# Scan of a state-space mixer: z projection between the heads, decays from running sums, norms per group

## The reference, cut to what matters

```
proj = u @ w_in                    # 256 x 5152: z 2048, xbc 3072, dt 32
xbc = silu(causal_dwconv(xbc, conv_w, conv_b))
xs, bm, cm = 32 heads x 64, 4 groups x 128, 4 groups x 128
dt = softplus(dt_raw + dt_bias);  a = -exp(a_log)
cs = cumsum(dt * a)                # per head, over time
y[l] = sum over s <= l of (cm[l] . bm[s]) * exp(cs[l] - cs[s]) * dt[s] * xs[s]
y = y + d_skip * xs
g = y * silu(z), normed by its mean square in each of 4 groups of 512
return (g * norm_w) @ w_out        # 2048 -> 1024
```

## Time and profile before

| what | value |
|---|---|
| median of 3 runs | 2651.09 us (2650.17 to 2657.0) |
| profiled execution | 2655.34 us, span 2653.6 us |
| PE busy | 2250.7 us, 85% of the span |
| DVE busy | 885.7 us, 33% |
| ACT busy | 364.8 us, 14% |
| DMA | 638 MB, 240 GB/s over the span |
| mixer, first z matmul to the last of the output product | 1501.32 to 1784.97 us |

### The profile page before, as it was taken

One profiled execution on the slowest core, in us unless ns is written; L12 is line 12 of the kernel. 1 busy time (PEld: TensorE's weight loads), 2 busy tenths in 40 slices (PEclk: granted clock), 3 DMA queues, 4 the chain that ended last, 5 costly groups with the idle time before them and its releaser, 6 DMA issues.

```text
span 2653.6 us, 28827 instructions
## 1 busy us (share of the span) xinstructions
PE 2250.7 (85%) x11598; PEld 1591.9 (60%) x11598; DVE 885.7 (33%) x1985; ACT 364.8 (14%) x740; POOL 1.2 (0%) x16
## 2 busy tenths in 40 slices
PE   6999999976666666667666799999999988899998
PEld 4877888832222222222222588687888877788886
DVE  6895994131000000100000226715231325333223
ACT  2231111120000000000000111302110114111111
POOL 0000000000000000000000000000000000000000
PEclk9999999988887788888878899999999989999999
DMA  7526563549999999999999742044444421454420
GB/s 267 178 96 213 200 223 126 236 195 429 427 428 429 429 428 430 428 429 429 429 429 428 266 159 96 1 142 143 159 158 146 142 98 62 155 175 147 157 95 16
DMA packets 147181, 638.03 MB, mean 240 GB/s; under 512 B 10245, under 2 KB 52750, under 8 KB 119198
## 3 DMA queue, kind: packets, MB, share of 16 engines
q1 hardware_dynamic: 146158, 634.79, 61.1%
q10 hardware_dynamic: 944, 2.13, 0.2%
HBM read 635.86 MB, written 1.05 MB: 240 GB/s over the span
## 4 chain that ended last, share of the span: by engine, by line
PE 69%; DMA 23%; DVE 5%; ACT 1%; issue 1%; SPq 0%; ACTq 0%; DVEq 0%
DMA arena<-in_w_down_dram 23%; PE PS L1520 17%; PE PS L1034 12%; PE PS L1533 8%; PE PS L947 8%; PE PS L1372 4%; PE PS L1274 3%; PE PS L1363 2%; PE PS L1399 2%; PE PS L958 2%; PE PS L1386 2%; DVE arena L1609 2%; PE PS L1282 1%; DVE rstd L1618 1%; PE PS L1466 1%
## 5 line engine op out<-in xcount | busy, mean ns | idle before, releaser
L1372 PE MATMUL PS<-arena,hT 128*32 128x512 f32 x2048 | 310.0, 749 | 163.7 <-DMA arena<-in_w_up_dram 137.9
L1520 PE MATMUL PS<-hT,arena 128*128 128x256 f32 x2048 | 444.5, 379 | 2.9 <-DVE hT L1609 2.9
L1520 PEld LDWEIGHTS PS<-hT,arena 128*128 128x128 f32 x2048 | 388.9, 190 | 56.6 <-issue 3.8
L1372 PEld LDWEIGHTS PS<-arena,hT 128*32 128x32 f32 x2048 | 66.8, 126 | 386.4 <-DMA arena<-in_w_up_dram 211.7
L1034 PE MATMUL PS<-hT,arena 128*128 128x256 f32 (+1 forms) x1136 | 253.7, 383 | 1.5 <-ACT hT L682 1.5
L1386 PE MATMUL PS<-arena,hT 128*32 128x512 f32 x1024 | 170.7, 804 | 98.2 <-DMA arena<-in_w_down_dram 90.3
L1609 DVE SCALAR_TENSOR_TENSOR arena<-arena 128x512 f32<-128x512 f32 (+2 forms) x514 | 246.5, 548 | 0.9
L1034 PEld LDWEIGHTS PS<-hT,arena 128*128 128x128 f32 (+1 forms) x1136 | 213.4, 190 | 39.4 <-issue 9.7
L1533 PE MATMUL PS<-arena 128*128 128x256 f32 x1024 | 223.3, 379 | 0.0
L1606 DVE TENSOR_SCALAR arena<-arena,cols 128x256 f32<-128x256 f32 x162 | 66.4, 410 | 465.0 <-ACT arena L879 380.4
L947 PE MATMUL PS<-hT,arena 128*128 128x256 f32 x960 | 214.0, 387 | 6.1 <-DVE hT L1609 6.1
(11 more groups left out here) (242 smaller groups left out, 1627.6 us busy)
## 6 DMA issues: line engine op xcount, KB each, us to landing
arena<-in_w_gate_dram SPq DMA_DIRECT2D x64, 2048.0 KB, 40.8
arena<-in_w_up_dram SPq DMA_DIRECT2D x64, 2048.0 KB, 40.7
arena<-in_w_down_dram SPq DMA_DIRECT2D x64, 2048.0 KB, 37.5
arena<-in_ffn_w_up_dram SPq DMA_DIRECT2D x32, 2048.0 KB, 8.7
arena<-in_w_in_dram SPq DMA_DIRECT2D x36, 1024.0 KB, 8.0
arena<-in_ffn_w_down_dram SPq DMA_DIRECT2D x16, 2048.0 KB, 8.0
arena<-in_w_ada_dram SPq DMA_DIRECT2D x12, 2048.0 KB, 11.6
arena<-in_ssd_w_in_dram SPq DMA_DIRECT2D x10, 2048.0 KB, 12.8
```

The source lines that it names most:

```text
L1372: mm = pe.matmul(PS[32 * f:32 * f + 32, 1 + half, :], xe[:, 32 * (2 * pi + k):32 * (2 * pi + k) + 32], w[:, k, 512 * f:512 * f + 512], sta ...
L1520: mm = pe.matmul(PS[:, n, T * half:T * half + T], slot(TAIL_SLOT[j], 8, 512)[:, k, P * n:P * n + P], hT[:, k, :], start=(k == 0), stop=(k ...
```

## The change

The order of the weights is dt, x, z, and so is PE's. dt comes first; dt, da and their running sums are made beside the x tiles. The tiles of x and z go through three PSUM banks instead of four (`ssd_tile`); the transposes of xs follow four by four behind the panels (`x_turn`), and so do their products with dt (`x_dt`). Running sums of da over time are made once, by five products with the triangular constant: `cs` with tokens on partitions, `csT` with the 32 heads twice on 64 partitions.

The heads run in 16 pairs. `decay` broadcasts the row of `csT` of each of the two heads over 128 partitions, by one product on 32 rows with a column of the identity as stationary operand, the two heads on different rows. `span` on DVE subtracts the other running sum and takes the minimum with zero, from PSUM into `em`; ACT takes exp of a pair at once, `weigh` on DVE multiplies a pair with `cb`; the masks are in `cb`. `head_out` does the two heads of a pair in turn, first both products of 256 columns and then both of 128. Between the decays of a pair and the output of the pair two before, PE has one z tile; ACT copies it out and takes silu of four together. Norm and squares of a group follow within the loop or, for group 3, within the output product, which now uses banks 0 to 3 and starts before the last two outputs of pairs. The norm behind the mixer changes its banks accordingly.

```diff
@@ -96,7 +96,7 @@
...
-TAIL = [("ssd_z", 4), ("ssd_dt", 1), ("ssd_x", 6), ("ssd_out", 4), ("ffn0", 25), ("lru_in", 5),
+TAIL = [("ssd_dt", 1), ("ssd_x", 6), ("ssd_z", 4), ("ssd_out", 4), ("ffn0", 25), ("lru_in", 5),
...
 def norm_bank(name):

-    return 3 if "post" in name or name in ("lat_q", "ffn1") else 7
+    if name == "ssd3":
+        return 4
+    return 3 if "post" in name and name != "mix_post0" or name in ("lat_q", "ffn1", "ssd0", "ssd1", "ssd2") else 7
...
-        td = [sq_[:, 384 * i:384 * i + 384] for i in range(4)]
-        em = [oa_[:, 384 * i:384 * i + 384] for i in range(3)]
+        em = [view(so_, 1024 + 768 * i, 2, 384) for i in range(3)]
+        csT, da2 = so_[0:64, 3328:3584], view(so_, 3584, 2, 64)
+        cs = view(so_, 3712, 2, SSD_H)
...
+            def z_copy(t):
+                act.wait_ge(*tile_done(s, used, "z_ps", ["ssd_x", "ssd_z"], NX + t))
+                act.activation(zs[:, t, :], PS[:, t % 3, 0:T], ACT.Copy).then_inc(s["z_ready"], 1)
+            def group_squares(g):
+                act.wait_ge(s["ss_ps"], NORM[f"ssd{g}"][0])
+                squares(f"ssd{g}", lambda p, n: zs[:, 4 * g + 2 * p:4 * g + 2 * p + 2, :],
+                        lambda p: ("yg_ready", 4 * g + 2 * p + 2))
+            z_copy(0)
+            for i in range(NZ):
+                act.wait_ge(s["d_ready"], i + 1)
+                act.activation(em[i % 3], em[i % 3], ACT.Exp).then_inc(s["e_ready"], 1)
+                if i % 4 == 3 and i >= 7:
+                    group_squares(i // 4 - 1)
+                if i + 1 < NZ:
+                    z_copy(i + 1)
+                if i % 4 == 2:
+                    g = i // 4
+                    act.wait_ge(s["z_ready"], 4 * g + 4)
+                    act.activation(zs[:, 4 * g:4 * g + 4, :], zs[:, 4 * g:4 * g + 4, :], ACT.Silu
+                                   ).then_inc(s["zs_ready"], 1)
+                if i % 4 == 0 and i >= 8:
+                    root(f"ssd{i // 4 - 2}")
+            root("ssd2")
+            group_squares(3)
+            root("ssd3")
...
-                mm = tile(PS[:, 4, 32 * c:32 * c + 32], [(hT[:, k, P * c:P * c + P], w[:, k, :]) for k in range(KD)])
+                mm = tile(PS[:, 4, 32 * c:32 * c + 32], [(hT[:, k, P * c:P * c + P], w[:, k, :]) for k in range(KD)],
+                          norm=None if c else "mix_pre0")
             mm.then_inc(used, ST.incs["ssd_dt"][0])
...
+            def ssd_tile(t):
+                name, j = ("ssd_x", t // 4) if t < NX else ("ssd_z", (t - NX) // 4)
+                if t % 4 == 0:
+                    arrived(name, j)
+                if 3 <= t < NX + 3:
+                    pe.wait_ge(s["xc_ev"], t - 2)
+                elif t >= NX + 3:
+                    pe.wait_ge(s["z_ready"], t - 2 - NX)
+                w = slot(ST.slots[name][j], 8, 512)
+                mm = tile(PS[:, t % 3, 0:T], [(w[:, k, P * (t % 4):P * (t % 4) + P], hT[:, k, :]) for k in range(KD)])
+                if t % 4 == 3:
+                    mm.then_inc(used, ST.incs[name][j])
+                else:
+                    mm.then_inc(s["z_ps"], 1)
+            def x_turn(q):
+                for c in range(TC):
+                    b = 2 * q + c
+                    pe.wait_ge(s["xbc_ready"], 4 * q + 4)
+                    if b >= 2:
+                        pe.wait_ge(s["xdt_ready"], b - 1)
+                    for u in range(4):
+                        mm = pe.transpose(PS[:, 5 + c, P * u:P * u + P], xbc[:, 4 * q + u, P * c:P * c + P], ident)
+                    mm.then_inc(s["xst_ps"], 1)
...
+                for n in range(4):
+                    ssd_tile(4 * j + n)
+                if 1 <= j <= 4:
+                    x_turn(j - 1)
+                if j == 3:
+                    pe.wait_ge(s["da_ready"], 1)
+                    pe.matmul(PS[0:64, 7, 0:T], da2[:, 0, :], tri_ones, start=True, stop=False, skip_group_check=True)
+                    pe.matmul(PS[0:64, 7, P:T], da2[:, 1, :], tri, start=False, stop=True, skip_group_check=True)
+                    pe.matmul(PS[:, 7, 256:288], tri, da[:, 0, :], start=True, stop=True)
+                    pe.matmul(PS[:, 7, 288:320], tri, da[:, 1, :], start=True, stop=False)
+                    pe.matmul(PS[:, 7, 288:320], ones, da[:, 0, :], start=False, stop=True).then_inc(s["cs_ps"], 1)
+            ssd_tile(NX)
             pe.wait_ge(s["xbc_ready"], NX)
+            pe.wait_ge(s["xdt_ready"], 8)
+            pe.wait_ge(s["cs_ready"], 2)
...
+                pe.matmul(PS[:, 4 + g, 0:T], B_[:, 0:P], C_, start=True, stop=True)
+                pe.matmul(PS[:, 4 + g, T:384], B_[:, P:T], C_[:, P:T], start=True, stop=True).then_inc(s["cb_ps"], 1)
+            def decay(p):
+                if p == 0:
+                    pe.wait_ge(s["cb_ready"], 4)
+                if p:
+                    pe.wait_ge(s["d_ready"], p)
+                for u in range(2):
+                    h, r = 2 * p + u, slice(32 * u, 32 * u + 32)
+                    mm = pe.matmul(PS[:, 4 + u, 0:T],
+                                   ident[r, 32 * u + h:32 * u + h + 1].broadcast_to([32, P]), csT[r, :],
+                                   start=True, stop=True)
+                    mm.then_inc(s["d_ps"], 1)
+            def head_out(p):
+                pe.wait_ge(s["m_ready"], p + 1)
+                if p == 0:
                     pe.wait_ge(s["cb_ready"], 2 * SSD_G)
-                if tt >= 4 and h % 2 == 0:
-                    pe.wait_ge(s["yg_tmp"], tt - 3)
-                r = slice(64 * (h % 2), 64 * (h % 2) + 64)
-                m = em[h % 3]
-                pe.matmul(PS[r, tt % 4, 0:T], xdt[:, 0, 64 * h:64 * h + 64], m[:, 0:T], start=True, stop=False,
-                          skip_group_check=True)
-                pe.matmul(PS[r, tt % 4, P:T], xdt[:, 1, 64 * h:64 * h + 64], m[:, T:384], start=False, stop=True,
-                          skip_group_check=True).then_inc(s["yh_ps"], 1)
-            pe.wait_ge(s["dt_ready"], 1)
-            for h in range(SSD_H + 2):
-                if h < SSD_H:
-                    decay(h)
-                if h >= 2:
-                    head_out(h - 2)
-            for g in range(SSD_G):
-                norm_pe(f"ssd{g}")
-            pe.wait_ge(s["std_ready"], NORM["ssd3"][0] + 1)
-            pe.wait_ge(s["e_ready"], SSD_H)
+                if p >= 2:
+                    pe.wait_ge(s["yg_tmp"], p - 1)
+                m, b = em[p % 3], 6 + p % 2
+                for u in range(2):
+                    h = 2 * p + u
+                    pe.matmul(PS[64 * u:64 * u + 64, b, 0:T], xdt[:, 0, 64 * h:64 * h + 64], m[:, u, 0:T],
+                              start=True, stop=False, skip_group_check=True)
+                for u in range(2):
+                    h = 2 * p + u
+                    mm = pe.matmul(PS[64 * u:64 * u + 64, b, P:T], xdt[:, 1, 64 * h:64 * h + 64],
+                                   m[:, u, T:384], start=False, stop=True, skip_group_check=True)
+                mm.then_inc(s["yh_ps"], 1)
+            for i in range(NZ):
+                decay(i)
+                if i + 1 < NZ:
+                    ssd_tile(NX + i + 1)
+                if i >= 2:
+                    head_out(i - 2)
+                if i % 4 == 3 and i >= 7:
+                    norm_pe(f"ssd{i // 4 - 1}")
+            pe.wait_ge(s["z_ready"], NZ)
+            pe.wait_ge(s["std_ready"], NORM["ssd2"][0] + 1)
+            open_rows(0)
             hr = NORM["ssd0"][3]
-            row_product([(("ssd_out", j), 4, (lambda k, j=j: zs[:, 4 * j + k, :]),
-                          (lambda k, j=j: [(s["h_ready"], hr + 4 * j + k + 1)])) for j in range(4)], 1)
+            for k in range(NZ):
+                j = k // 4
+                if k % 4 == 0:
+                    arrived("ssd_out", j)
+                w = slot(ST.slots["ssd_out"][j], 4, D)
+                pe.wait_ge(s["h_ready"], hr + k + 1)
+                for n in range(KD):
+                    mm = pe.matmul(PS[:, n // 2, T * (n % 2):T * (n % 2) + T], w[:, k % 4, P * n:P * n + P],
+                                   zs[:, k, :], start=False, stop=False, skip_group_check=True)
+                if k % 4 == 3:
+                    mm.then_inc(used, ST.incs["ssd_out"][j])
+                if k < 2:
+                    head_out(14 + k)
+                if k == 6:
+                    norm_pe("ssd3")
+            close_rows(0)
...
+            for c in range(TC):
+                ins = dve.tensor_copy(da2[:, c, :].rearrange("p (r h) -> p r h", r=2),
+                                      da[:, c:c + 1, :].broadcast_to([P, 2, SSD_H]))
+            ins.then_inc(s["da_ready"], 1)
+            def x_dt(q):
+                for c in range(TC):
+                    dve.wait_ge(s["xst_ps"], 2 * q + c + 1)
+                    tt(xdt[:, c, 512 * q:512 * q + 512].rearrange("p (h n) -> p h n", n=64),
+                       PS[:, 5 + c, :].rearrange("p (h n) -> p h n", n=64),
```

(72 more changed lines are left out.)

102 lines of the change are left out of this document (26 added, 76 removed).

## The result

The changed kernel takes 2622.39 us, median of 4 runs (2620.63 to 2623.47), against 2651.45 us (2650.17 to 2657.0) of the kernel before in the same comparison: a ratio of 0.9886, interval 0.9869 to 0.9903, 29.1 us less. Forecast were 2620.3 and 30.8 less. The profiled execution took 2620.63 us, 34.7 less than that of before, which lay 4.3 above its median. First the page of the changed kernel, which answers to the earlier trace rows.

The account below looks back on a forecast made before the run. TensorE was taken to own the state-space mixer stage almost alone. Terms from front to tail and output product summed to 252.8 us, 30.8 less than 283.65, giving a median of 2620.3 us, range 2611 to 2635.

Parts of the forecast that it names:

- Front: Start of the mixer stage: dt, waits for hT and low clock cost 8.2 us, against 6.9 before.
- Transposes and sums: x phase: 32 transposes between panels and five running-sum products add 5.5 us (4.8 to 6.5) on TensorE.
- Decays: Loop of pairs: two products on different row groups overlap, 0.65 us a pair with the shape change.
- Outputs: Loop of pairs: neighbouring heads use different column halves and overlap, 0.87 us a pair (0.75 to 1.5).
- z tile: Loop of pairs: one z tile between decays and output, 3.456 us plus 0.15 for the change of shape.
- The Trainium skill's rule: Loop: changing tiling mode drains the engine; read strictly, 48 x 0.25 = 12 us instead of 8, time 2624.
- Tail: From last decay to opening of the output product's banks: 7.5 us (6 to 10), where 15 were spent before.
- The low clock there: Tail: TensorE idles some 4 us, then a stretch at clock 0.50 costs 1.7 us.
- VectorE "over 80% busy in the loop": Loop of pairs: a sign to look for, with VectorE's work forecast at 4.2 to 4.4 us a pair.
- Rival (a): Loop: packing fails, decays and outputs go in series and shape changes cost more; time 2632, chance 0.16.
- Rival (b): Loop: VectorE or the chain through ScalarE's table loads sets the pair, 6.2 us; time 2638, chance 0.11.
- Rival (c): Loop: narrow mixed work keeps the clock at 1.2 GHz, up to 160 us; time 2700, slower, chance 0.04.

Follow-up runs that it names:

- e1: Changed kernel with both decay products of a pair reading the same rows, 0 to 31: 2627.50 us, ratio 0.9915 to the kernel before.
- e2: Changed kernel with a pair's outputs split, even head ahead of the z tile, odd head behind it: 2632.89 us, ratio 0.9937 to the kernel before.
- e8: Changed kernel with the decays of the kernel before, running sums left out: 2645.43 us (2640.4 without a disturbed execution), ratio 0.9962 to the kernel before.
- after_again: The changed kernel itself, unedited, timed and profiled a second time: 2621.89 us, ratio 0.9888 to the kernel before.
- e3: Changed kernel with all 16 z tiles ahead of the loop of pairs: 2659.14 us, ratio 1.003 to the kernel before.
- e4: Changed kernel with all four group norms behind the last output and the output product behind them: 2630.13 us, ratio 0.9917 to the kernel before.
- e5: Changed kernel with the two dt tiles behind the first and second x tile: 2618.26 us, ratio 0.9876 to the kernel before.
- e6: Changed kernel with group 2's squares ahead of the last exp, z's last silu behind group 2's root: 2619.48 us, ratio 0.9881 to the kernel before.
- e7: Changed kernel with both the dt move of e5 and the ScalarE reorder of e6: 2616.21 us, ratio 0.987 to the kernel before.
- e9: Kernel before with two decays issued, then the outputs of the two heads before, as neighbours: 2637.73 us, ratio 0.9952 to the kernel before.

## Why the prediction was right

The sum was 252.8 us for the stage; the two profiles have 249.8 and 252.6. No term was far off, and the mechanism, two overlaps on TensorE in a loop that TensorE sets, is the one that the runs show. By its own terms:

- Front, 8.2: measured 8.6. The second half of dt ran at 1.2 GHz to its end, as taken, and the x tiles for some 3 us more. The reason given was too short: 3.06 us of idle weren't all that went before the low clock. It had been 0.50 already from about 1491 to 1498, behind an idle of 4.18 us, and TensorE had run only sixteen issues of a norm since.
- Transposes and sums, 5.5: measured 4 x 0.87 + 1.6 = 5.1. The copy, conv and silu behind the last x tile were covered by z tile 0.
- Decays 0.65 a pair: 0.63. Outputs 0.87: 0.80. z tile 3.6: 3.65. The turn was forecast at 5.1 and is 5.08; the loop to the last decay, 79.9 with 13 outputs, is 79.0. The sign that it named, the second decay's first issue within 0.1 us of the first's, is there too (see e1). e1 and e2 show that the two overlaps carry it, which before could show only for 8 columns and for one place in 32 heads.
- The Trainium skill's rule that a change of tiling mode drains the engine ("TensorEngine Tiling (Array Packing)", section Tiling Modes) fits in that a change costs time. In this case's traces three changes a turn show 0.20, 0.19 and 0.15 us, and e8 removes one of them and its 0.19; the strict reading, 0.25 each, isn't borne out.
- Waits for the squares in the loop, 0.3 each: none, the norms took 1.93.
- Tail 7.5 us: 6.9. The low clock there, 1.7, was counted as sure: absent in the first profile, 2.9 in the second. Of the ten profiles with a changed loop six have a low clock between the last decay and the first issues of the product (after_again, e1, e3, e4, e5, e6) and four have none (the first one, e2, e7, e8). That term was a chance of about one half to pay 1.4 to 2.9.
- VectorE "over 80% busy in the loop" was wrong: 50.4 of 79.7 us, 63%. I had laid a norm on every fourth pair, while only two of four fall in the loop, and had added mean durations of operations that overlap. One of these was too short besides: a subtraction on 256 columns takes 0.48 us and not 0.42.
- Rival (a), no overlap: e1 and e2, added, price it at 0.43 + 0.8 a turn, 18 us. Rival (b): no, the turn is the sum of TensorE's own work. Rival (c): no in this kernel, where the clock is 1.00 through the loop; a low clock in the loop does come when the z tiles are taken away (e3). That the dt issues bring the clock down, on which it leaned, holds for one execution and not for another: in e9 it stayed at 1.00 behind them.

That 2620.3 lies so close to the median of 2622.39 is in part luck. By the same reckoning a stage of 249.8 us would have given 2617.3, and the median lies 5.1 us above that; a stage taken 3.0 us too long made up for more than half of it.

What the sum did not say, since it went by parts of the new order, is where the gain lies: by the table above in decays and outputs, with e8 (15.1) and e9 (13.8 in the loop) as witnesses from both sides. That z between the heads gains little by itself is argued and not shown: TensorE had no gaps to fill in the loop of before (48.36 of 50 us busy), and e8, with old decays and everything else new, has a stage only 1.8 us shorter than e9, the kernel before with paired outputs (some 5 us, had e9's front run at 0.50 as that of before did). No run moves z alone in the kernel before. In the new kernel z keeps the loop on TensorE and at 2.4 GHz now that decays and outputs alone would leave it waiting; its removal costs 39 us of the stage (e3). How much of the 39 is the clock and how much VectorE, no run separates.

Median and profile differ (29.1 and 34.7 us) because the profiled execution of before lies 3.9 us above its median in this comparison and that of the changed kernel 1.8 below its own. Executions vary outside the stage, in the same code: ahead of it by 5.4 us in these profiles (it starts between 1495.9 and 1501.3), behind it by 7.1 (868.4 to 875.6). That is why I judge edits of this stage by its own length first.

## What to carry to other kernels

Look in the trace for matmuls that use half the columns or a quarter of the rows and stand alone between full ones: making two of them neighbours on different columns or rows costs a line and here gave 13 us for the columns (e9) and about 6.5 us for the rows (e1). When such work gets cheap, another engine is next, here VectorE at 3.02 us a pair (e3), and with TensorE waiting its clock fell besides; full tiles between such work kept TensorE busy and its clock at 1.00. Price a dependency chain by the distance between starts of its operations, not by their mean durations.

## What the runs showed of the hardware

The clock near narrow work, always the same 32 issues of 32 moving columns: behind full tiles in the kernel before they took 3.65 us, with the clock at 0.50 behind them; in e9, with the same order, they took the same 3.65 us and the clock stayed at 1.00. At the head of the stage in the changed kernel they took 7.0 us, in part because the first half waits chunk by chunk for hT, and the clock stayed at 0.50 to their end. In two halves between full tiles (e5, e7) they took 1.87 us each, with the clock at 1.00.

The same program can fall on either side. Ahead of the stage TensorE idles 4.18 us, makes a norm in which the clock is 0.50 for 3 to 7 us, and idles 3.06 us more, in all profiles; the front then ran at 0.50 at least in part in all but two, and at 1.00 in e7 and e9. In the tail of the changed kernel TensorE idles 3.38 us ahead of the last norm; the clock stayed at 1.00 in the first profile and was 0.59 over 1685 to 1690 in the second. A shorter idle is no safety: in e6, with 1.58 us ahead of the opening, it fell to 0.50 at 1688.7, and in e7, with the same order there, it stayed. Why a given execution falls on one side was not settled.
